# Four softmax attentions of a two-part transformer kernel, re-staged as a pipeline of head pairs

## What is computed

```python
# first block
qa, ka, va, qb, kb, vb, gate_logits = split(h @ w_in)       # mod = silu(c) @ w_ada + b_ada feeds norms and gates
oa = moba_attention(qa, ka, va, rel_bias)                    # softmax, 8 heads, causal, "moba"
ob = stick_breaking_attention(qb, kb, vb)                    # no softmax
# even layer
a_q, a_k, a_v, b_q, b_k, b_v, i_q, i_k, i_w = split(h @ even_w_in)
p = softmax(a_q a_k); w = p[first] - lam * p[second]         # "mask": 4 heads with two softmaxes each
o_a = rmsnorm(w @ a_v)
idx = top_k(sum_h relu(i_q i_k) * i_w, 64)                   # the 64 best keys of each query
o_b = softmax over idx(b_q b_k) @ b_v                        # "sel", 8 heads
x = x + rmsnorm(concat(o_a, o_b) @ even_w_out)
# odd layer: 16 heads over a band of chunks, in two halves of 8: "odd0", "odd1"
```

## Time and profile before

| | |
|---|---|
| median of 3 runs | 1498.01 us (1497.97 to 1501.21) |
| the profiled execution | 1496.0 us |
| its span | 1494.2 us |
| mean granted PE clock | 0.986 |
| PE busy | 1420.8 us, 95% of the span |
| DVE busy | 894.2 us, 60% |
| ACT busy | 748.2 us, 50% |
| POOL busy | 82.6 us, 6% |
| HBM read | 272.05 MB, 183 GB/s over the span |

### The profile page before, as it was taken

The page is one execution under the profiler, slowest core; times in us unless marked ns, Lnnn a source line. Parts: engine busy times, 40 slices in busy tenths (PEclk is TensorE's granted clock), DMA queues, the critical chain, the costliest instruction groups (busy, mean ns, idle before and its releaser), DMA issues.

```text
span 1494.2 us, 18003 instructions
## 1 busy us (share of the span) xinstructions
PE 1420.8 (95%) x6775; PEld 1167.7 (78%) x6775; DVE 894.2 (60%) x1125; ACT 748.2 (50%) x1039; POOL 82.6 (6%) x133
## 2 busy tenths in 40 slices
PE   5999998999999999998799999999999999999998
PEld 4878877778877888876577888878888778778886
DVE  5577775788775554467746655456544454665543
ACT  4557735646545434355466543445344466564442
POOL 3011100000000000031200000000000100000000
PEclk9999999999999999999799999999999999999999
DMA  9787644467553766444224855638565363465650
GB/s 355 272 301 232 204 150 163 160 235 251 199 169 121 234 195 197 146 141 143 69 85 155 281 175 192 193 104 267 184 194 177 132 209 113 133 221 198 195 169 29
DMA packets 177446, 274.29 MB, mean 184 GB/s; under 512 B 6449, under 2 KB 120881, under 8 KB 177361
## 3 DMA queue, kind: packets, MB, share of 16 engines
q1 hardware_dynamic: 170656, 250.87, 50.8%
q0 software_dynamic: 5552, 20.20, 4.3%
q10 hardware_dynamic: 1153, 2.07, 0.4%
HBM read 272.05 MB, written 1.06 MB: 183 GB/s over the span
## 4 chain that ended last, share of the span: by engine, by line
PE 68%; DVE 8%; issue 3%; ACT 3%; DMA 1%; POOL 0%; DVEq 0%; SPq 0%; POOLq 0%; ACTq 0%
PE psum L2212 21%; PE psum L2214 21%; PE psum L2213 21%; DVE w_lo L1839 2%; PE psum L2413 2%; DVE PR L2151 1%; DMA raw<-in_w_up_dram 1%; ACT w_hi L1637 1%; DVE scr L2174 1%; PE psum L2288 1%; ACT attn L1757 0%; PE psum L2342 0%; PE psum L2341 0%; PE psum L2357 0%; DVE lo_qk L1839 0%
## 5 line engine op out<-in xcount | busy, mean ns | idle before, releaser
L1839 DVE TENSOR_TENSOR w_lo<-raw,w_hi 128x2048 fp32r<-128x2048 f32 (+1 forms) x158 | 358.6, 2273 | 213.0 <-ACT w_hi L1637 212.6
L2212 PE MATMUL psum<-w_hi,hT_hi 128*128 128x512 f32 x1000 | 400.9, 401 | 19.7 <-DVE w_lo L1839 8.5
L2214 PE MATMUL psum<-w_hi,hT_lo 128*128 128x512 f32 x1000 | 392.0, 392 | 0.0
L2213 PE MATMUL psum<-w_lo,hT_hi 128*128 128x512 f32 x1000 | 391.1, 391 | 0.0
L1637 ACT ACTIVATE w_hi<-raw 128x2048 fp32r<-128x2048 f32 (+1 forms) x158 | 300.0, 1901 | 136.6 <-PE psum L2214 92.4
L2212 PEld LDWEIGHTS psum<-w_hi,hT_hi 128*128 128x128 f32 x1000 | 189.6, 190 | 64.8 <-issue 17.5
L2214 PEld LDWEIGHTS psum<-w_hi,hT_lo 128*128 128x128 f32 x1000 | 189.0, 189 | 40.5
L2213 PEld LDWEIGHTS psum<-w_lo,hT_hi 128*128 128x128 f32 x1000 | 189.6, 190 | 37.0 <-issue 0.5
L1839 DVE TENSOR_TENSOR lo_qk<-raw,hi_qk 128x2048 fp32r<-128x2048 f32 (+1 forms) x35 | 79.3, 2264 | 41.5 <-ACT hi_qk L1637 41.5
L2212 PE MATMUL psum<-w_hi,hc_hi 128*128 128x512 f32 x256 | 101.0, 395 | 1.8 <-DVE hc_lo L1844 1.1
L1839 DVE TENSOR_TENSOR lo_at<-raw,hi_at 128x2048 fp32r<-128x2048 f32 x35 | 80.1, 2290 | 34.8 <-ACT hi_at L1637 34.7
(11 more groups left out here) (207 smaller groups left out, 2014.2 us busy)
## 6 DMA issues: line engine op xcount, KB each, us to landing
raw<-in_ffn_wg_dram SPq DMA_DIRECT2D x88, 512.0 KB, 4.0
raw<-in_ffn_wu_dram SPq DMA_DIRECT2D x88, 512.0 KB, 5.0
raw<-in_ffn_wd_dram SPq DMA_DIRECT2D x44, 1024.0 KB, 4.9
raw<-in_w_up_dram SPq DMA_DIRECT2D x44, 512.0 KB, 5.0
raw<-in_w_in_dram SPq DMA_DIRECT2D x19, 1024.0 KB, 7.7
ada_raw<-in_w_ada_dram POOLq DMA_DIRECT2D x24, 512.0 KB, 5.2
raw<-in_even_w_in_dram SPq DMA_DIRECT2D x12, 1024.0 KB, 5.1
raw<-in_odd_w_in_dram SPq DMA_DIRECT2D x12, 1024.0 KB, 5.2
```

The lines of the kernel that those rows point to most:

```text
L1839: nc.vector.tensor_tensor(lo_of(s), raw_of(s), hi_of(s).bitcast(F32), ALU.subtract).then_inc(lo_ready, 1)
L2212: nc.tensor.matmul(o, a_hi, b_hi, start=start, stop=False)
L2213: nc.tensor.matmul(o, a_hi, b_lo, start=False, stop=False)
L2214: return nc.tensor.matmul(o, a_lo, b_hi, start=False, stop=stop)
```

## The change

`softmax_heads` is replaced by `softmax_pairs`, which runs a chain of pairs of one or more attentions. In step i the order is: `ahead` fillers, `qk` of pair i, `mix` of pair i-1, `dense` fillers, `exp` of pair i, `late` fillers, `pv` of pair i-2, `probturn` of pair i-1, `end` fillers. In the last step `pv` of pair i-2 and `probturn` of pair i-1 come ahead of the dense fillers, and `pv` of pair i-1 behind them. The products of a projection and its `projout` become separate fillers. The transposes of queries and keys go to banks 2 and 3 instead of 6 and 7. In the even layer the whole third projection (the values of "sel", two units) moves from "sel" into the last step of "mask", and `diffout` is split by tile. The odd layer's two attentions become one chain of 8 pairs. The first 12 matmuls of the second output half (`out_second`) move from behind the last `pv` to ahead of it, and split the units of the output projection to its last.

```diff
+        for i in range(n + 1):
+            filler("ahead")
+            if i < n:
+                qk(*pairs[i])
+            if i and pairs[i - 1][0]["diff"]:
+                pl.add("mix", n=pairs[i - 1][0]["n0"] + 2 * pairs[i - 1][1] + 1)
+            if i == n:
+                pv(*pairs[i - 2])
+                probturn(*pairs[i - 1])
+            filler("dense")
+            if i < n:
+                exp(*pairs[i])
+            filler("late")
+            if i == n:
+                pv(*pairs[i - 1])
+            else:
+                if i >= 2:
+                    pv(*pairs[i - 2])
+                if i:
+                    probturn(*pairs[i - 1])
+            filler("end")
...
-    fa = [[sum_next, quarter, f] for name in ("qb", "kb", "vb") for f in heads_of[name]]
-    fa += [[sum_next, turn_second], [quarter], [sum_next]]
+    fa = [((), [sum_next, qb[0]], [quarter]),
+          ((), [sum_next, qb[1]], [quarter, qb[2]]),
+          ((), [sum_next, kb[0]], [quarter]),
+          ((), [sum_next, turn_qb, kb[1]], [quarter, kb[2]]),
+          ((), [sum_next, turn_kb, vb[0]], [quarter], [sum_next, quarter, vb[3], sum_next, quarter, sum_next])]
...
+        def out_second(w):
+            def go():
+                outs[1] = [pl.use(2), pl.use(3, by_unit=True)]
+                outs["p"] = out_unit(w, 1, 0)
+                pl.split_to(outs["p"]["unit"] + 2)
+                product_step("proj", outs["p"], ts=(0,), inc=None)
+            return go
...
-            fills = [[first_of(3), topk(0)], [second_of, topk(1)], [topk(2), rope_of(3, "bq")],
-                     [first_of(4), topk(3)], [second_of, topk(4)],
-                     [fill_turn(3, "bq", 8), topk(5)],
-                     [topk(6)], [topk(7), rope_of(4, "bk")], [], [fill_turn(4, "bk", 12)]]
+            topk(0)[0]()
+            fills = [((), [first_of(3)], topk(1, 2)),
+                     ((), [second_of], [finish] + topk(3)),
+                     ((), [first_of(4)], topk(4) + [rope_of(3, "bq")]),
+                     ((), [turn_of(3, "bq", 8), second_of], [finish] + topk(5, 6)),
+                     ((), [first_of(5), second_of], [finish] + topk(7) + [rope_of(4, "bk")])]
+            softmax_pairs([diff], fills)
+            turn_of(4, "bk", 12)()
+            diff_out(0)()
-            fills = [[first_of(5)], [second_of, diff_var], [diff_norm(0)], [diff_norm(1)], [turn_first("scr", ("scr_ready", v))],
-                     [out_first(W["even_w_out"][0])]]
+            fills = [((), (), [diff_out(1)]),
+                     ((), (), [diff_var]),
+                     ((), (), [lambda: diff_norm(0)(), lambda: diff_norm(1)()]),
+                     ((), (), [lambda: turn_first("scr", ("scr_ready", scr_version()))()], [out_first(W["even_w_out"][0])]),
+                     ((), [out_second(W["even_w_out"][0])])]
...
+            fills = [((), [odd_first(1)]),
+                     ((), [odd_second], [finish]),
+                     ((), [odd_first(3)]),
+                     ((), [turn_of(1, "pq", 8), odd_second], [finish]),
+                     ([odd_start(5, (0,)), turn_of(3, "pk", 12), odd_go_on((1,), None)], [odd_go_on((2, 3), "unit")]),
+                     ((), [odd_second], [finish]),
+                     ((), (), (), [lambda: turn_first("pr", ("uses", first["o"]))()]),
+                     ((), [out_first(W["odd_w_out"][0])]),
+                     ((), [out_second(W["odd_w_out"][0])])]
+            softmax_pairs([first, second], fills)
```

More of the change, by code:

```diff
@@ L402, in head_turn, with attention @@
         return use
[L404 removed]
+    def attention(bias, v_col, v_w, q_ready, v_ready, diff=False, base=0, done=None):
         n0 = n_attn[0]
         n_attn[0] += 8
[L409 to L455 removed]
@@ L1176, in build_plan, with turn_of, finish, topk @@
-            n0, o = softmax_heads(fills, "mask", 2 * BANK, 2 * HD, q_ready_of("aq", "ak"), lambda: u2,
-                                  diff=True)
+            def turn_of(i, nm, blk):
+                return lambda: turns_of(nm, i, blk, 2, ("rope_ready", held[nm]))
+            def finish():
+                pl.add("projout", ts=(0, 1), **held["parts"][1])
+            def topk(*js):
+                return [lambda j=j: pl.add("topk", j=j) for j in js]
+            topk(0)[0]()
             sd = pl.new_stat(8)
-            pl.add("diffout", uses=o, st=sd, n0=n0)
@@ L1194, in build_plan @@
+            softmax_pairs([sel], fills)
             out_rest("scr", W["even_w_out"][0], norm_chain(1.0), ffn)
```

182 lines of the change are left out of this document (93 added, 89 removed).

## The result

| | before | changed |
|---|---|---|
| median | 1497.99 us (1496.16 to 1501.21, 4 runs) | 1516.51 us (1513.74 to 1518.48, 4 runs) |
| ratio, 95% interval | | 1.012 (1.0096 to 1.0144) |
| span of the profiled execution | 1494.2 us | 1515.5 us |
| PE busy | 1420.8 us | 1431.8 us, 94% |
| mean granted PE clock | 0.986 | 0.979 |

The change makes the kernel 18.5 us slower. The forecast was 1506.5 us, the range ended at 1515. The direction was right and the size was not. (The two profiled executions, from which all that follows is read, lie 21.3 us apart: 1517.3 and 1496.0.)

A forecast was written before the change was run, and what follows sets the result against it. The prediction took PE, with 68% of the chain, as the bound. Its terms, 13 - 2 - 1.5 - 1.8 = +7.7, about 8 to 9 with small waits, took the profiled 1496.0 to 1504.5 and the median to 1506.5 us; range 1495 to 1515.

The forecast's parts named there:

- Part 1: In moba, quarters spaced anew make the chain of load and quarter set the pace: +13 us, bounds +8 and +18.
- parts 2 and 3: Mask wins `mix` waits but takes two units; sel loses those products: together about -2 us, bounds -8 and +6.
- part 4: Odd's single chain of eight pairs, -1.5 us, and the early split in `out_second` ending the `w_lo` waits, -1.8.
- small waits: Waits for bank 3 in moba and odd, raising the sum from +7.7 to about 8 to 9 us.
- The clock falls ... so about 2 us of work are lost: In moba behind the 7.1 us wait for quarter 8: a slow clock put at 4 us, losing about 2.
- the walk: Step-by-step timing of PE and the other queues: stick-breaking `sb_z` at 152.8, sel's first `qk` at 747.5, sel 31 us.
- I take 2.66 for both places: In mask, steps 2 and 4: `mix` beside POOL's rope takes 2.66 us; with 0.75 this part is 4 better.
- PE works at the slow clock for 2 us or so of lost time: In sel, after the first `pv`, which comes 9.8 us behind `bk`'s copies while PE has 3.5 us of work.
- rival D: Sel runs on the slow clock between `bk`'s copies and the first `pv`: 8 us on top of A, 1514; chance 0.15.
- A: The forecast itself, 1506.5 us: the chain of quarters ends in the open, with PE waiting for it; chance 0.52.
- The signs named: Trace signs for being right: two `adasum` waits, `mix` waits about 3 us, mask's clock above 0.80, sel idle 7 to 9.
- Rival B: Mask truly wins the `mix` waits and slow clock, part 1 costs at most 4: about 1485 us; chance 0.19.

The follow-up runs named there:

- moba_old: The changed kernel with only the first block's attention (moba) staged as in the kernel before, one quarter in each filler: 1499.72 us, ratio 1.0022.
- quarters: The changed kernel with its pair pipeline kept and only the first block's quarters and sums of rows set at other places: 1501.25 us, ratio 1.0038.
- warm: The changed kernel with 26 extra matmuls of 256 columns on PE ahead of each of three sums of rows that wait for a quarter: 1514.29 us.
- quarter_first: The changed kernel with only the quarters of the first block's first two steps moved ahead of the unit and its split: 1512.75 us, ratio 1.0109.
- sel_warm: The changed kernel with 16 extra matmuls ahead of the first group of `bk` transposes and 16 ahead of sel's first `pv`: 1514.21 us, ratio 1.0104.
- mo_undo: `moba_old` with `out_second` fully undone, its 12 matmuls and its splits behind the last `pv` again: 1495.93 us, ratio 0.9993.
- best2: `mo_even2` plus halved `out_second` matmuls, `bq` transposes behind the unit, and output projection's starting transposes ahead of `exp` in sel and odd: 1485.42 us, ratio 0.9910.
- mo_even2: `moba_old` with the third projection's second unit back in sel, and last `topk` and rope of `bk` ahead of its first unit: 1495.29 us, ratio 0.9987.

## Why the prediction was wrong in size

The stages of the two traces differ by 20.9 us, and the prediction's sum was 8 to 9. Part 1 came out 4.5 us above its term, parts 2 and 3 together 2.6, part 4 4.2, and 1.9 came in a stage that had no term; against them stand the 0.8 that had been added for small waits. The steps that failed are these: in part 1 the load ahead of the second quarter and the number of falls of the clock; in part 3 the slow clock and the waits of sel; in part 4 a saving in odd that no row carried, and a split that `out_second` moved ahead of `o_evac` on DVE.

**Part 1, moba: +13, measured +17.5.** The mechanism was right: the chain of load and quarter, 7.5 and 6.8 us for the last two (133.24, 140.70, 147.52) against 7.2 and some tenths. `moba_old` and `quarters` show it. Two sizes were wrong.
The first wait was put at "about 2 us" and was 3.73: the load of the second quarter's first half, issued at 81.68, was used at 89.33, 7.6 us later, where 5.66 were taken. This was no accident of one execution: the same load took 7.6 to 8.0 us from issue to use in the four kernels that have this order of the first two quarters, and 5.2 to 5.8 in the nine others, where it was issued some 2.2 us sooner in the stage. What it met there was not tried. And no clock was charged for that wait; `warm` shows 1.00 in place of 0.58 there. Together they account for quarter 5 at 125.35 instead of 122.3, and all behind it came 3.2 to 3.8 us late, quarter 8 at 147.52 instead of 144.3.
The step "The clock falls ... so about 2 us of work are lost" counted one fall where there are three. From the last sum to the second `sb_z` it took 9.6 us instead of the walk's 8.5; at full clock the kernel before needs 6.6 for the same (132.70 to 139.26). 3.3 and 1.1 make the 4.4 us between the walk's 152.8 and the 157.2 measured. The fall behind the second wait cost nothing, as the chain ended the third wait anyhow.
The load's price by the Trainium skill ("DMA: Bandwidth & Descriptors", "Anatomy of one DMA"), 3.2 us by its formula, is not borne out here either: the 24 loads of `ada_raw` in the changed kernel took 4.1 to 7.6 us, with a median of 5.1.

**Parts 2 and 3: -2, measured +0.6.** Mask came out as walked: sel's first `qk` at 766.76, which is 747.0 in the time of the kernel before (mask began 19.74 later), against 747.5. That is luck, since two errors cancel in it. "I take 2.66 for both places" held for the first place and, in this trace, not for the second:

```profile
732.51 2.81 DVE L2104 SCALAR_TENSOR_TENSOR attn<-attn,rsum 128x128 f32<-128x128 f32 x2
...
749.43 0.75 DVE L2104 SCALAR_TENSOR_TENSOR attn<-attn,rsum 128x128 f32<-128x128 f32 x2
```

No wait for `mix` stands in the list of PE's waits here. The other error is in the waits for the two ropes, 2.8 and 2.0 instead of 1.4 and 1.6:

```profile
PE psum L2377 <- DVE PR L2036: 4.8, 2, 2.8
```

(Waits of PE in mask and sel of the changed kernel: total, times, longest.) In `quarters` and `quarter_first`, with the same code in mask, the second place was slow as well (2.71 us): PE waited 2.94 us for it, where the walk had 2.5. The waits for the ropes were still 2.7 to 2.8 and 2.0, and mask took 55.3 and 55.9 us, where the walk had 53.6. So the order of the list alone does not settle which price of `mix` holds.

Sel took 34.0 instead of 31, and two things failed in the walk. "PE works at the slow clock for 2 us or so of lost time" was too little: the clock cost 3.0 us, 34.0 against the 31.0 of `sel_warm`. But the walk's 31 has its 2 us of slow clock inside, so without them it is 29, and at full clock sel still takes 31.0. So 2 us more lie in its other terms. 1.1 of them are two waits in `sel_warm`, 1.6 for the turned halves (said 1.1) and 2.0 for `o_evac` (said 1.4); the rest isn't taken apart, and PE has smaller waits of 0.3 to 0.7 us in front of `qk` and `probturn` besides. The slow clock is rival D at its place, at 3 us and not 8. It was priced as another world than A; both came true, and A with D's real price would have ended the forecast higher. The rule of the Trainium skill that stood beside D ("TensorE: Matmul & The Clock Gate", "A second HAM failure mode: psum-queue depth-cycling") says that short idle times between groups of matmuls bring the clock down again and again. The trace agrees that it falls in such a stretch: 0.50 with PE busy for 5.8 of the 8 us in the row of 772 to 780 above. That it comes and goes with each group is not what the row shows; it stayed down.

**Part 4: -1.5 and -1.8, measured +1.5 and about -0.6.** The waits that the prediction names add up to +1.0 (1.5 saved, 1.1 and 1.4 lost); the way from there to -1.5 is carried by the two `exp` rounds over products alone, for which it has no number. That step failed: the pipeline in odd is worth -0.6 by `mo_undo`, where `o_evac` is not held up. The stretch had 2.2 us of idle time and its clock at 1.00, and can't give back more than that; `best2` gets just these 2.2 (71.0 to 68.8). The new wait for `o_evac` was put at 1.4, the wait itself; it was 2.0, in both layers, and the clock fell behind one of the two. In the changed kernel it was the second (0.57 for 4 us), which ate the wait for `w_lo` won there, so that "to the end" is 0.6 longer while "to odd" is 1.2 shorter; in `quarters`, `quarter_first` and `mo_even2`, with the same code there, it was the first (0.66 over 5 us), and "to the end" is 1.1 shorter than before. What I didn't see is that the split stands ahead of `o_evac` on DVE; I named the queues for POOL and SP, and not for this step.

**The signs named.** Waits in front of the sums behind moba: 3.3 and 3.6 (said 2.6 and 7). The second is shorter because PE's work between the two sums took 10.7 us at the slow clock instead of the walk's 7.6; in `warm`, at full clock, it took 7.5, and 6.5 us were left until the quarter was done. Waits for `mix` near zero (said 3; 2.9 in `quarters` and `quarter_first`). Clock of mask 0.92. Sel's idle time 7.2 us, 34.0 less 26.8 (said 7 to 9), but only some 3 us of it ended by ACT and the rest by DVE (said ACT). The wait of 0.9 for `w_lo` is gone. Rival B, true winnings in mask, was right that the mixes would be free and wrong that nothing would take their place.

Open: why the clock fell at 222 to 226 us in the changed kernel (0.57), and not in the kernel before behind the same two waits of PE of 0.8 and 1.2 us. It makes up most of the +1.9 "to mask" and was not tried by itself. In the same code the stretch from the second `sb_z` to the sum of the last row took 84.7 us in seven of the thirteen kernels and 83.1 in six, so it is no property of the change. Open too is why the load of the second quarter took 2 us more when it was issued later.

## What to carry to other kernels

When side work runs as a chain of its own (load, use, load again), walk its times against those of the path after any re-spacing; its pace, not its amount, decides, and a first link begun late shifts all of them. Charge an idle time of PE twice, once for the wait and once for the slow clock that may follow it, unless something else ends last there anyhow. When a matmul is moved, look at what its splits are moved past on the other engines; and never give a stretch more gain than its idle time and its slow clock hold.

## What the runs showed of the hardware

- 26 matmuls of 256 columns in the place of a wait kept the clock at 1.00 (92 to 96 us in `warm`), and 16 ahead of the transposes of `bk` and 16 ahead of the first `pv` kept all of sel there in `sel_warm` and made it 3.0 us shorter.
- Where the matmuls did not reach to the end of the wait, the clock fell all the same: at the third sum of `warm` 26 of them left 2.5 us open, and it was 0.57 from 146 to 150 us.
- The same wait does not always cost a slow clock. Eight of these kernels wait 1.9 to 2.0 us for `o_evac` once in sel and once in odd, and in each trace the clock fell behind only one of the two: behind the one in odd in five (1.00 at 801 to 806 and 0.57 at 1304 to 1308 in the changed kernel), behind the one in sel in three (0.66 and 1.00 in `quarters`). It cost about 1.5 us in either place.
- `mix` took 2.7 to 2.8 us where the whole of it lay beside the rope on POOL, and 0.75 beside none, as in the earlier trace rows; in the kernel before one that met only the rope's end took 1.68 (733.65). The last one in mask, beside the start of the rope of `bk`, was either: 0.75 at 749.43 in the changed kernel, where POOL began at 749.83, and 2.71 at 733.58 in `quarters`, where POOL had begun at 732.26. A split that did overlap took 3.43 instead of 2.29 us (at 753.83).
- From the sum of the last row to mask, identical code, single executions took between 469.6 and 475.2 us. A difference of 3 us in a whole span from one profile each says nothing. In a single stage it says something when several traces of the same code agree, or when the waits and the clock in it account for the difference; sel alone took 32.6 to 34.0 us in six traces of the same products.
